# First layer's output projection as split fp32r products, with Pool, ACT and DVE making the halves

## The reference, cut to what matters

```python
proj = rmsnorm(h, norm_mix_even[i]) @ w_in_ab[i]
ssd_out = ssd_mixer(...)                 # 512 columns, normalised in two groups
attn_out = diff_attention(...)           # 512 columns, 4 heads, normalised per head
h = h + jnp.concatenate([ssd_out, attn_out], axis=-1) @ w_out_ab[i]
h = h + swiglu(rmsnorm(h, norm_ffn_even[i]), ffn_w_gate[i], ffn_w_up[i], ffn_w_down[i])
```

## Time and profile before

| | us |
|---|---|
| Median of 3 runs (1522.82 to 1527.17) | 1527.09 |
| The profiled execution, its own time | 1525.42 |
| Its span | 1523.8 |
| PE busy in it | 1496.6 |
| DVE busy | 717.2 |
| ACT busy | 310.8 |
| POOL busy | 90.9 |

### The profile page before, as it was taken

One profiled execution on the slowest core, in us unless ns is written; L12 is line 12 of the kernel. 1 busy time (PEld: TensorE's weight loads), 2 busy tenths in 40 slices (PEclk: granted clock), 3 DMA queues, 4 the chain that ended last, 5 costly groups with the idle time before them and its releaser, 6 DMA issues.

```text
span 1523.8 us, 45002 instructions
## 1 busy us (share of the span) xinstructions
PE 1496.6 (98%) x19964; PEld 1214.2 (80%) x19964; DVE 717.2 (47%) x1730; ACT 310.8 (20%) x498; POOL 90.9 (6%) x93
## 2 busy tenths in 40 slices
PE   8999999999999999999999999999999999999997
PEld 6776599999988887777777777778877777777785
DVE  5478456665488854322523533432523433433433
ACT  3375344443436502000000000000000000000002
POOL 0061000000034420000000000000000000000000
PEclk9999999999999999999999999999999999999998
DMA  9322055567423444999999999999999999999991
GB/s 287 114 83 82 3 165 166 168 207 224 147 83 111 139 167 178 394 393 391 393 392 390 386 389 392 381 391 390 385 390 388 387 387 390 388 384 391 387 387 59
DMA packets 221538, 431.60 MB, mean 283 GB/s; under 512 B 9546, under 2 KB 76624, under 8 KB 221040
## 3 DMA queue, kind: packets, MB, share of 16 engines
q1 hardware_dynamic: 218104, 425.34, 76.5%
q10 hardware_dynamic: 3256, 3.54, 0.7%
HBM read 427.80 MB, written 1.05 MB: 281 GB/s over the span
## 4 chain that ended last, share of the span: by engine, by line
PE 94%; DVE 4%; ACT 1%; issue 1%; DMA 0%; ACTq 0%; DVEq 0%
PE ps L1690 92%; PE ps L1707 1%; DVE arena L1084 1%; DVE ring_lo L1291 1%; DVE arena L1225 0%; DMA ktab<-in_k_table_dram 0%; ACT ring_hi L888 0%; DVE arena L1168 0%; DVE arena L1166 0%; ACT arena L701 0%; DVE arena L1193 0%; DVE arena L1199 0%; DVE xtk_lo L1508 0%; DVE arena L1194 0%; DVE arena L1200 0%
## 5 line engine op out<-in xcount | busy, mean ns | idle before, releaser
L1690 PE MATMUL ps<-raw,xg 128*32 128x384 f32 (+2 forms) x9216 | 525.6, 379 | 0.0
L1690 PEld LDWEIGHTS ps<-raw,xg 128*32 128x32 f32 x9216 | 390.6, 110 | 115.0 <-ACT xg L1009 0.2
L1558 DVE STREAM_TRANSPOSE ehT<-eh 32x96 f32<-32x96 f32 x896 | 241.7, 270 | 62.0 <-PE ps L1690 32.1
L1690 PE MATMUL ps<-raw,ehT 128*32 128x384 f32 (+2 forms) x4608 | 267.6, 379 | 0.0
L1546 DVE TENSOR_TENSOR eh<-esg,ps 128x384 f32<-128x384 f32 x56 | 31.1, 555 | 499.1 <-PE ps L1690 480.4
L1690 PEld LDWEIGHTS ps<-raw,ehT 128*32 128x32 f32 x4608 | 202.7, 110 | 49.7 <-issue 0.2
L1003 ACT ACTIVATE esg<-ps 128x384 f32<-128x384 f32 x56 | 27.3, 488 | 672.9 <-PE ps L1690 672.9
L1690 PE MATMUL ps<-xn_hi,ring_hi 128*128 128x272 f32 x544 | 160.8, 296 | 0.9 <-DVE ring_lo L1291 0.9
L1690 PE MATMUL ps<-xn_hi,ring_lo 128*128 128x272 f32 x544 | 158.7, 292 | 0.0
L1690 PE MATMUL ps<-xn_lo,ring_hi 128*128 128x272 f32 x544 | 158.0, 290 | 0.0
L1690 PE MATMUL ps<-xn,ring 128*128 128x272 f32 (+1 forms) x640 | 156.6, 405 | 0.9 <-DVE xn L1084 0.8
(11 more groups left out here) (299 smaller groups left out, 1187.4 us busy)
## 6 DMA issues: line engine op xcount, KB each, us to landing
raw<-in_moe_w_gate_dram SPq DMA_DIRECT2D x96, 1024.0 KB, 16.0
raw<-in_moe_w_up_dram SPq DMA_DIRECT2D x96, 1024.0 KB, 15.2
raw<-in_moe_w_down_dram SPq DMA_DIRECT2D x96, 1024.0 KB, 14.0
raw_ring<-in_moe_w_down_dram SPq DMA_DIRECT2D x16, 1024.0 KB, 14.2
raw_ring<-in_moe_w_gate_dram SPq DMA_DIRECT2D x16, 1024.0 KB, 15.7
raw_ring<-in_moe_w_up_dram SPq DMA_DIRECT2D x16, 1024.0 KB, 15.6
ring<-in_w_in_ab_dram SPq DMA_DIRECT2D x12, 1024.0 KB, 6.7
ring<-in_hy_w_in_dram SPq DMA_DIRECT2D x12, 1024.0 KB, 5.0
```

Of the source, the lines that this page charges most:

```text
L1558: V.transpose(ehT[GROUP * q:GROUP * q + GROUP, s % 2, g, :, :], src).then_inc(sem("ehT_ready"), 1)
L1690: return nc.tensor.matmul(o, l, r, start=start, stop=stop)
```

## The change

The output projection is made with `product`. ACT makes the high halves of its four weight blocks (`wo_high`, new), POOL subtracts to get the low halves, in place of the ring slot, and the eight mixed columns are cut by ACT (high) and DVE (`cat_low`, new). The high halves of the blocks get three buffers (the fourth block reuses the first) laid over parts of the arena that are free by then. Some semaphores are merged (`squares3` into `squares2`, `xn3_ready` into `xn2_ready`, `coef_ready` into `v_ready`), with counts moved accordingly.

The diff, cut to its core:

```diff
@@ buffers @@
+        cat_hi, cat_lo = overlay("cat_hi", 4384, KT, T), overlay("cat_lo", 6560, KT, T)
+        wo_hi = [overlay(f"wo_hi{i}", at, 256 * KT) for i, at in enumerate((8736, 1536, 11552))]
@@ POOL, behind the last by_cos and ahead of the filter's work @@
+            for i in range(4):
+                pool.wait_ge(sem("wo_high"), i + 1)
+                n = B_WO + i
+                g(nc.gpsimd.tensor_tensor(ring_lo[:, n % RING, 0:256 * KT], ring[:, n % RING, 0:256 * KT], wo_hi[i % 3][:].bitcast(F32), ALU.subtract), sem("wo_low"))
...
-            pool.wait_ge(sem("coef_ready"), 1)
-            pool.wait_ge(sem("v_ready"), 1)
+            pool.wait_ge(sem("v_ready"), 2)
@@ ACT @@
+            def wo_high(i):
+                n = B_WO + i
+                act.wait_ge(slot_in[n % RING], 16 * (n // RING + 1))
+                if i == 2:
+                    act.wait_ge(used("at"), 12)
+                    act.wait_ge(used("o"), 4)
+                nc.scalar.activation(wo_hi[i % 3][:], ring[:, n % RING, 0:256 * KT], ACT.Copy).then_inc(sem("wo_high"), 1)
...
                 copy("vt", tt, vT[0:n, tt, :], n, slice(0, 512))
+            wo_high(0)
+            wo_high(1)
             turned_map(0)
...
-            act.wait_ge(sem("cat_ready"), 8)
+            wo_high(2)
             for k in range(KT):
+                act.wait_ge(sem("cat_ready"), k + 1)
+                nc.scalar.activation(cat_hi[:, k, :], cat[:, k, :], ACT.Copy).then_inc(sem("cat_high"), 1)
+            for k in range(KT):
+                if k == 2:
+                    wo_high(3)
                 weighted_high(k, C_NFE)
                 squares("wo", "squares2", k)
                 if k == 3:
@@ DVE @@
+            def cat_low(k):
+                dve.wait_ge(sem("cat_high"), k + 1)
+                V.tensor_tensor(cat_lo[:, k, :], cat[:, k, :], cat_hi[:, k, :].bitcast(F32), ALU.subtract).then_inc(sem("cat_low"), 1)
+
+            for k in range(4):
+                cat_low(k)
             dve.wait_ge(used("ns"), 2)
             v(V.reciprocal(csr[0:4, 1, :], csr[0:4, 1, :]), sem("norm_rows"))
             for k in range(4):
                 t = ready(dve, "nb", 2 + k)
                 mult_add(cat[:, 4 + k, :], osb[:, k, :], lam[:, 5:6], t[:, 0:T], sem("cat_ready"), ALU.mult, ALU.mult)
                 V.memset(crd[:, 8:9], 0.0).then_inc(used("nb"), 1)
+                if k:
+                    cat_low(3 + k)
+            cat_low(7)
@@ PE @@
             def out_columns(j, part):
-                n = B_WO + j // 2
+                i = j // 2
+                n = B_WO + i
                 if part == 0:
-                    if j % 2 == 0:
-                        arrived(n)
+                    pe.wait_ge(sem("wo_low"), i + 1)
                     open_tile("wo", j)
...
                     if j == 0:
-                        pe.wait_ge(sem("cat_ready"), k + 1)
-                    last = mm(o[:, 0:T], slot(n)[:, k, P * (j % 2):P * (j % 2) + P], cat[:, k, :], k == 0, k == KT - 1)
+                        pe.wait_ge(sem("cat_low"), k + 1)
+                    last = product(o[:, 0:T], high[:, k, c], low[:, k, c], (cat_hi[:, k, :], cat_lo[:, k, :]), k == 0, k == KT - 1)
...
-            add_squares("ss2", "squares2", 0, 2)
-            linear("wo", 4, B_WO + 2, cat)
-            add_squares("ss2", "squares2", 2, 2)
-            linear("wo", 6, B_WO + 3, cat)
+            add_squares("ss2", 0, 0, 2)
+            for j in (4, 5):
+                out_columns(j, 0)
+                out_columns(j, 1)
+            add_squares("ss2", 0, 2, 2)
+            for j in (6, 7):
+                out_columns(j, 0)
+                out_columns(j, 1)
```

More of the change, by code:

```diff
@@ L941, in _ @@
                     for k in (d - 1, d):
-                        squares("down", "squares3", k)
+                        squares("down", "squares2", k)
             ring_high(B_HY + 1)
@@ L1368, in _ @@
                     for k in (d - 2, d - 1):
-                        weighted_low(k, C_NMO, "xn3_ready", KT)
+                        weighted_low(k, C_NMO, "xn2_ready", KT)
             for k in (6, 7):
-                weighted_low(k, C_NMO, "xn3_ready", KT)
+                weighted_low(k, C_NMO, "xn2_ready", KT)
             dve.wait_ge(sem("filter_in"), 112)
@@ L1422, in _ @@
                     v(V.reciprocal(invn, t[:, 0:8]), used("kn"))
-                    v(V.tensor_tensor(coefn, coef, invn.rearrange("p (k a) -> p k a", a=1).to_broadcast([P, KT, META]), ALU.mult), sem("coef_ready"))
+                    v(V.tensor_tensor(coefn, coef, invn.rearrange("p (k a) -> p k a", a=1).to_broadcast([P, KT, META]), ALU.mult), sem("v_ready"))
                 if m == 8:
@@ L1734, in add_squares @@
                 for k in range(k0, k0 + n):
-                    pe.wait_ge(sem(s), k + 1)
+                    pe.wait_ge(sem("squares2"), s + k + 1)
                     last = mm(o[:, 0:toks.stop - toks.start], ones[:], sq[:, k, toks], k == 0, k == KT - 1)
@@ L1913, in out_columns @@
             def out_columns(j, part):
-                n = B_WO + j // 2
+                i = j // 2
+                n = B_WO + i
                 if part == 0:
-                    if j % 2 == 0:
-                        arrived(n)
+                    pe.wait_ge(sem("wo_low"), i + 1)
                     open_tile("wo", j)
-                o = ps[NUMBER[("wo", j)] % 8]
+                o, c = ps[NUMBER[("wo", j)] % 8], slice(P * (j % 2), P * (j % 2) + P)
+                high, low = [a.rearrange("p (k n) -> p k n", k=KT) for a in (wo_hi[i % 3][:], ring_lo[:, n % RING, 0:256 * KT])]
                 for k in range(4 * part, 4 * part + 4):
                     if j == 0:
-                        pe.wait_ge(sem("cat_ready"), k + 1)
-                    last = mm(o[:, 0:T], slot(n)[:, k, P * (j % 2):P * (j % 2) + P], cat[:, k, :], k == 0, k == KT - 1)
+                        pe.wait_ge(sem("cat_low"), k + 1)
+                    last = product(o[:, 0:T], high[:, k, c], low[:, k, c], (cat_hi[:, k, :], cat_lo[:, k, :]), k == 0, k == KT - 1)
                 if part:
@@ L1969, in swiglu_columns @@
                             if first and c == 0 and part == 0 and j == 0 and k == KT - 1:
-                                add_squares("ss2", "squares2", 4, 4)
+                                add_squares("ss2", 0, 4, 4)
                                 pe.wait_ge(sem("xn2_ready"), KT)
@@ L1999, in _ @@
                 if b:
-                    add_squares("ss3", "squares3", 2 * b - 2, 2)
+                    add_squares("ss3", KT, 2 * b - 2, 2)
             pe.wait_ge(sem("sin_ready"), 3)
@@ L2042, in in_columns @@
                         if m == 0 and j == 0:
-                            pe.wait_ge(sem("xn3_ready"), k + 1)
+                            pe.wait_ge(sem("xn2_ready"), KT + k + 1)
                         c = slice(P * j, P * j + P)
@@ L2052, in _ @@
             for k in (6, 7):
-                pe.wait_ge(sem("squares3"), k + 1)
+                pe.wait_ge(sem("squares2"), KT + k + 1)
                 last = mm(o[:, 0:T], ones[:], sq[:, k, :], False, k == KT - 1)
@@ L2068, in _ @@
                 if m >= 10:
-                    pe.wait_ge(sem("v_ready"), 3)
+                    pe.wait_ge(sem("v_ready"), 4)
                     for k, rows in enumerate((v_plus, v_minus, hyc[:, 8:16, META + P:T])):
```

## The result

The changed kernel takes 1538.84 us (median of 4 runs, 1537.58 to 1543.85) where the kernel before takes 1527.13 (1522.82 to 1527.26). The ratio is 1.0093, with a 95% interval from 1.0073 to 1.0113, or 11 to 17 us. The direction is the one forecast and the median lies in the range of 1528 to 1540. The size was forecast at 9.0 us; by the ratio it is 14.2. The forecast of 1534.4 us was built on the profiled execution of before (1525.42 us), and its counterpart, the profiled execution of the changed kernel, took 1543.85 us: 18.4 us more, twice the forecast, and outside the range.

A forecast was written before the change was run, and what follows sets the result against it. PE, busy 98% of the span, was taken as the bound, with ACT, PE and DVE alternating in the attention. Attention 6.3, projection start 2.7 and clock 0 gave +9.0 us on 1525.42, so 1534.4 us, range 1528 to 1540.

The forecast's parts named there:

- PE's work, minus 4.4 us: Output projection: 64 contractions as three fp32r matmuls each go from 28.5 to 24.1 us.
- ACT in the attention, plus 3.06 us: Attention: two high halves (3.82 us) queued on ACT, less 0.76 us idle, delay head 2's exponentials by 3.06 us.
- POOL against DVE: Attention, head 2: POOL's 4.6 us subtractions exclude DVE's instructions for whole instructions, costing 3.2 us.
- Rival 1: POOL and DVE don't exclude each other at 2048 columns with fp32r output: 1526.6 or 1523.1 us; chance 0.13.
- rival 2: One of the two POOL and DVE exclusions falls away: 1530 to 1531 us; chance 0.12.
- The stall in the attention: PE idle some 5.7 us ahead of values(1), which starts 6.3 us later: 3.1 from ACT, 3.2 from exclusion.
- The start of the projection: Ahead of out_columns(0, 0): PE idle 7.7 us; with work saved and small gaps, this part costs 2.7 us.
- What costs nothing: Later projection: wo_high(3) and wo_low(3) are hidden behind tiles 2 to 5, and DVE's delayed low halves catch up.
- The clock: Attention and projection: two half-clock stretches stay, 3.5 us, adding 0; bounded by none (minus 3.5) and four (plus 3.5).
- Rival 3: More slow clock: both stalls draw half-clock stretches and the old two stay, 1537.9 us; chance 0.12.

The follow-up runs named there:

- e8_best: Changed kernel with ACT's first four mixed-column high halves earlier, blocks 0 and 1 high halves in ACT's idle time, low halves 0 to 2 on DVE: 1518.60 us, 0.9953.
- the reordering alone: Changed kernel with ACT's first four high halves of mixed columns ahead of the root and block 2's high half: 1529.09 us, ratio 1.0022.
- e2_fill: Changed kernel plus 50 unread bfloat16 matmuls on zeros in PE's three waits (before values(0), values(1) and the projection): 1538.93 us.
- e1_again: The changed kernel once more, no edit, with its own trace: 1538.82 us, ratio 1.0099.
- e3_act_only: Kernel before plus only two unused high halves on ACT ahead of turned_map(0), projection still float32: 1526.74 us, ratio 1.0001.

## Why the prediction was right or wrong

- **PE's work, minus 4.4 us: right.** With the same two stretches of half clock (6.8 us) the projection took 5.1 us less in e8_best, where the prediction has 4.4 and 0.6 of small gaps.
- **ACT in the attention, plus 3.06 us: right in mechanism, a little large.** DVE's first `combine` of head 2 starts 9.93 us behind the first mark instead of 7.19, so 2.74 later: the two high halves took 3.71 us and not 3.82, and the three copies behind them 1.22 and not 1.37. The idle time of 3.06 us ahead of it in DVE's row above is another quantity (0.32 before), and its likeness to the forecast is chance.
- **POOL against DVE: right**, in mechanism and size. 4.6 us for a subtraction: 4.50 to 4.62. The tensor_scalar, which no row of before had shown beside POOL, is blocked too: 3.58 us instead of 0.36, so 3.2. By the Trainium skill, SBUF — State Buffer, Who interferes with whom, a DVE instruction in a 2-port mode or with two SBUF inputs contends with a GpSimd instruction that reads SBUF, and the lock is exclusive. The trace agrees for two SBUF inputs (4.585 us), and for the tensor_scalar (3.58 us) if it ran in such a mode, which no run shows. Rival 1 and rival 2 are out.
- **The stall in the attention: right in sum, wrong in place.** `values(1)` starts 16.4 us behind the first mark instead of 10.5, so 5.95 later where 6.3 was forecast. But the prediction has one stall of 5.7 us ahead of `values(1)` and none ahead of `values(0)`, whose copies stand on ACT behind the high halves too. The trace has 2.25 us ahead of `values(0)` and 1.91 ahead of `values(1)`, and the clock falls 1.0 us behind the end of the first.
- **The start of the projection: right.** PE idle 7.7 us, measured 7.60; the reordering alone takes it away.
- **What costs nothing: right.** `wo_low(3)` held a low half of the stream for 4.55 us, and PE had no wait for it.
- **The clock: this step failed.** "I keep two, 3.5 us, and bound the term by none (minus 3.5) and four (plus 3.5)." There are four, but 17.1, 3.4, 10.2 and 3.4 us long: 34.1 us at 1.2 GHz, not 6.8 or 13.6. I had taken the length of the stretches of before for a property of a stretch. The price: the prediction's count at full clock gives 66.4 us up to the SwiGLU (60.9, less the 3.5 of slow clock in it, plus the 9.0), the trace 76.3. So about 9.9 us go to half clock, where 3.5 was put: 4.1 in the attention, 1.7 in the norms, 4.1 in the projection. The missing 6.4 us are the difference between 9.0 and the 15.4 measured. Rival 3 named this, but with 3.5 us more. That the median of the changed kernel lies in the range all the same is luck: the range reached to 1540 for rival 3, four stretches of 3.4 us, which is not what the trace shows.
- **What e2_fill says of that price.** Its projection, all at 2.4 GHz, took 28.3 us against 32.3, so 4.0 less, close to the 4.1 counted. In the attention `values(1)` starts 16.4 us behind the first mark in both kernels, at either clock; from there to the second mark it is 15.3 us in the changed kernel, 12.6 in e2_fill (with 3.2 us at 1.2 GHz left) and 10.9 before. So half clock cost 4.4 us there, and the 4.1 of the count are short by the 0.35 that the waits were shorter than forecast.
- **What is not shown: why a stretch begins and ends where it does.** The waits account for the long ones, since filling them took these away. But the clock of before falls at 181.6 us although PE had had no gap since 168.5, and in the changed kernel it stays low for 5.6 us of products without a gap. So no rule for the length comes out of these runs.
- On the Trainium skill's clock rule (TensorE: Matmul & The Clock Gate, Part 1), which I had called weakly contradicted: e2_fill agrees with its first half, that an idle engine falls to 1.2 GHz. PE kept busy in its waits held 2.4 GHz for 19 us; the changed kernel ran at 1.2 GHz for 17.1 us of the same stage. The row at 10 us in the earlier trace rows was one quiet microsecond and should not have been weighed against it. The fall at 181.6 us behind 13 us without a gap is a case that the rule doesn't explain.

## What to carry to other kernels

Before moving elementwise work to GpSimd, look what VectorE does in those microseconds: each of its instructions with two SBUF inputs, and its fast tensor_scalar, may wait for a whole GpSimd instruction (here 3.2 and 4.2 us on the critical path for 4.5 us of work); where nobody waits it is harmless, as the 4.55 us in e8_best. Work that prepares a saving of 4.4 us on TensorE is paid in the queue where it stands: in ACT's and DVE's idle time, with only one subtraction left on GpSimd, it turned plus 13 us into minus 7. And a stall of TensorE can cost more than its length: here the slow clock around two short waits and one long one lasted 17.1 and 10.2 us. The stretches of the kernel before (3.4 us each) don't price it; filling the waits once, as in e2_fill, shows it.

## What the runs showed that I had not expected

- Between the marks the stretches at 1.2 GHz repeat from run to run, in length and place, in one kernel (34.1 us in both traces of the changed kernel); there they are no noise. Outside of the marks they do differ (17.1 us in the changed kernel between the SwiGLU's start and 700 us, 10.2 in e1_again).
- Fillers ahead of 191 us changed the clock at 451 to 595 us in three traces of two kernels: 1318.3 to 1318.4 us from the SwiGLU's start to the end, against 1312.3 to 1315.8 in all others. The slow clock goes with it: between the SwiGLU's start and 700 us those three traces have 23.9 us at 1.2 GHz, all others 10.2 to 17.1. A stall filled in one stage was paid in another, and the total stayed. The cause is open.
- Half clock costs nothing while another engine sets the pace. Of the 17.1 us stretch the first 7.8, up to `values(1)`, are free, since that start is set by DVE's `head_out(0)`; the 9.3 us behind it cost 4.4 (15.3 us to the second mark instead of 10.9). In e3_act_only, where DVE is ready 3.2 us earlier, the same part is not free: `values(1)` is late by the clock and has no wait.
